# Experts' tokens gathered for two experts at a time, from high and low parts made by POOL, and the next expert's first gate product put between the two halves of the scatter

## What is computed

```python
def moe_swiglu(h, w_router, w_gate, w_up, w_down):
    logits = (h @ w_router).astype(jnp.float32)
    top_val, top_idx = lax.top_k(logits, TOP_K)              # 2 of 8
    top_w = jax.nn.softmax(top_val, axis=-1)
    gates = jnp.sum(jax.nn.one_hot(top_idx, N_EXPERTS) * top_w[..., None], axis=-2)
    out = jnp.zeros_like(h)
    for e in range(N_EXPERTS):
        y = (jax.nn.silu(h @ w_gate[e]) * (h @ w_up[e])) @ w_down[e]
        out = out + gates[..., e:e + 1] * y
    return out
```

## Time and profile before

| what | value |
|---|---|
| runs | 1834.43, 1839.47, 1834.2 us (median 1834.43) |
| profiled execution | 1839.33 us |
| its span | 1837.6 us, mean granted clock 0.989 |
| busy, of the span | PE 98%, DVE 76%, ACT 62%, POOL 6% |
| the experts' stage | from about 461 to 1448 us of the span |
| weights read | 476 MB by SP's queue |

### The profile page before, as it was taken

One profiled execution on the slowest core, in us unless ns is written; L12 is line 12 of the kernel. 1 busy time (PEld: TensorE's weight loads), 2 busy tenths in 40 slices (PEclk: granted clock), 3 DMA queues, 4 the chain that ended last, 5 costly groups with the idle time before them and its releaser, 6 DMA issues.

```text
span 1837.6 us, 25765 instructions
## 1 busy us (share of the span) xinstructions
PE 1794.9 (98%) x9992; PEld 1551.8 (84%) x9992; DVE 1405.8 (76%) x1164; ACT 1131.7 (62%) x942; POOL 116.7 (6%) x133
## 2 busy tenths in 40 slices
PE   8999999999999999999999999999999898899999
PEld 6789999898888888888888888888888797689998
DVE  6475445655988989898889888898898867677775
ACT  6444444463776777777777777767677544645553
POOL 7000000000000000000000000000000028210000
PEclk9999999999999999999999999999999999789999
DMA  7446565432998998998989989989999543225561
GB/s 234 161 139 196 172 206 183 161 138 81 356 386 310 388 367 323 385 369 324 375 329 375 368 321 385 368 327 381 343 355 370 199 141 135 69 86 189 184 200 54
DMA packets 244356, 479.27 MB, mean 261 GB/s; under 512 B 11759, under 2 KB 80137, under 8 KB 244249
## 3 DMA queue, kind: packets, MB, share of 16 engines
q1 hardware_dynamic: 243385, 476.43, 72.3%
q10 hardware_dynamic: 864, 1.31, 0.2%
HBM read 476.66 MB, written 1.05 MB: 260 GB/s over the span
## 4 chain that ended last, share of the span: by engine, by line
PE 89%; DVE 5%; POOL 2%; ACT 2%; issue 1%; DMA 0%; DVEq 0%; ACTq 0%; SPq 0%; POOLq 0%
PE bank L1978 28%; PE bank L1980 27%; PE bank L1979 27%; PE bank L2297 1%; PE bank L2329 1%; POOL arena L820 1%; DVE wl L438 1%; DVE xT L1295 1%; DVE xTl L1238 1%; POOL arena L821 1%; PE bank L2366 0%; PE bank L1947 0%; PE bank L2367 0%; DVE h L1308 0%; DVE xn L1251 0%
## 5 line engine op out<-in xcount | busy, mean ns | idle before, releaser
L1978 PE MATMUL bank<-wh,xTh 128*128 128x512 f32 x1568 | 622.2, 397 | 11.1 <-DVE arena L1334 5.4
L1980 PE MATMUL bank<-wh,xTl 128*128 128x512 f32 x1568 | 613.1, 391 | 0.0
L1979 PE MATMUL bank<-wl,xTh 128*128 128x512 f32 x1568 | 612.5, 391 | 0.0
L1542 DVE TENSOR_TENSOR wl<-raw,wh 128x2048 fp32r<-128x2048 f32 x224 | 512.1, 2290 | 92.6 <-ACT wh L1024 91.0
L1024 ACT ACTIVATE wh<-raw 128x2048 fp32r<-128x2048 f32 x224 | 429.2, 1918 | 120.7 <-PE bank L1980 120.7
L1978 PEld LDWEIGHTS bank<-wh,xTh 128*128 128x128 f32 x1568 | 295.8, 189 | 74.2 <-DVE arena L1334 5.6
L1980 PEld LDWEIGHTS bank<-wh,xTl 128*128 128x128 f32 x1568 | 295.6, 189 | 62.9
L1979 PEld LDWEIGHTS bank<-wl,xTh 128*128 128x128 f32 x1568 | 296.1, 189 | 58.6
L438 DVE TENSOR_TENSOR wl<-raw,wh 128x2048 fp32r<-128x2048 f32 x112 | 255.4, 2298 | 68.3 <-ACT wh L431 66.5
L1978 PE MATMUL bank<-xTh,wh 128*128 128x256 f32 x1024 | 292.1, 285 | 1.2 <-DVE xTl L1238 0.8
L1980 PE MATMUL bank<-xTh,wl 128*128 128x256 f32 x1024 | 290.9, 284 | 0.0
(11 more groups left out here) (379 smaller groups left out, 1397.3 us busy)
## 6 DMA issues: line engine op xcount, KB each, us to landing
raw<-in_moe_w_up SPq DMA_DIRECT2D x112, 1024.0 KB, 7.6
arena<-in_moe_w_gate SPq DMA_DIRECT2D x96, 1024.0 KB, 7.5
raw<-in_moe_w_down SPq DMA_DIRECT2D x96, 1024.0 KB, 7.1
raw<-in_w_up SPq DMA_DIRECT2D x22, 1024.0 KB, 5.8
raw<-in_moe_w_gate SPq DMA_DIRECT2D x16, 1024.0 KB, 7.4
arena<-in_moe_w_down SPq DMA_DIRECT2D x16, 1024.0 KB, 7.2
raw<-in_gla_w_in SPq DMA_DIRECT2D x12, 1024.0 KB, 8.0
raw<-in_w_in SPq DMA_DIRECT2D x12, 1024.0 KB, 6.2
```

Of the source, the lines that this page charges most:

```text
L1542: V.tensor_tensor(wl[:, s, :], moe_raw(c)[0], wh[:, s, :].bitcast(F32), ALU.subtract).then_inc(lo_moe, 1)
L1978: T.matmul(o, xh, yh, start=first, stop=False)
L1979: T.matmul(o, xh, yl, start=False, stop=False)
L1980: return T.matmul(o, xl, yh, start=False, stop=last)
```

## The change

- `oh` becomes `oh2`, which holds the one-hot matrices of two experts side by side (`slots(i)` picks one) in fp32r; the type is that of a second view `arena_r` of the same memory.
- POOL gets three new operations of 128 x 2048 right after the first gathers (`moe_xgfull` at 2): `xnh` is the tokens times the gain, as fp32r; `xn` is multiplied by the gain in place; `xnl` is `xn` minus `xnh`. The gain's row comes by a new DMA of 512 KB on ACT's queue, ahead of the one for `fgain`.
- `gather_pair` replaces the 14 later calls of `gather`. It runs once in a pair, after down of round 5 of the pair's first expert (i = 0), and makes the tokens of that pair's second expert and of the next pair's first: 4 banks x 2 channel blocks x 2 token tiles x (high, low), 32 fp32r matmuls of 128x256. It runs in the last pair too. The gain is in the operands already, so ACT and DVE split each bank straight from PSUM (four operations of 128x512 each, in a pair).
- The activations' high and low parts move from `xTh`/`xTl` to the arena.
- On PE the next expert's gate of round 0 moves from behind the scatter to between its halves. On DVE the last low part of an expert (`weights_lo(UC - 1)`) moves ahead of the last two additions to `h`.

```diff
@@ -74,7 +74,7 @@
         h = sb("h", [P, TT, D])
-        with nc.sbuf_tensor("ohT", [P, S], F32R) as ohT:
+        with nc.sbuf_tensor("xnh", [P, TT, D], F32R) as xnh:
@@ -84,7 +84,11 @@
         yh, yl = (a.rearrange("p a n -> p (a n)").rearrange("p (k s) -> p k s", s=S) for a in (acth, actl))
+        with nc.sbuf_tensor("xnl", [P, TT, D], F32R) as xnl:
+            pass
...
         xn = sb("xn", [P, TT, D])
+        with nc.sbuf_tensor("arena_r", [P, AR], F32R) as arena_r:
+            pass
@@ -122,6 +126,10 @@
+        def ar_r(n):
+            ar(n)
+            return arena_r[:, ar_at[0] - n:ar_at[0]]
@@ -453,6 +461,7 @@
         lo_moe = sg("lo_moe")
+        pair_banks = (0, 2, 3, 7)
@@ -528,15 +537,21 @@
         more_i = ar(1).bitcast(I32)
-        oh = ar(TT * P).rearrange("p (t s) -> p t s", t=TT)
+        oh2 = ar_r(TT * 2 * P).rearrange("p (t s) -> p t s", t=TT)
+        ohT = ar_r(S)
...
         ghot, gnow = ar(1), ar(TT)
-        xg = ar(KD * P).rearrange("p (k s) -> p k s", k=KD)
-        xgh, xgl = xTh[:, :, 0:P], xTl[:, :, 0:P]
-        eactTh, eactTl = xTh[:, :, P:S], xTl[:, :, P:S]
+        eactTh, eactTl = (ar_r(KD * P).rearrange("p (k s) -> p k s", k=KD) for _ in range(2))
+        gainrow = rs_home[:, 0:D]
...
         junk = arena[:, ar_at[0] - D:ar_at[0]]
-        assert 2 * EJ == D
+        assert 2 * EJ == D == KD * P
+        xg = junk.rearrange("p (k s) -> p k s", k=KD)
+        def slots(i):
+            return slice((1 - i % 2) * P, (2 - i % 2) * P)
@@ -799,6 +814,13 @@
             pool.wait_ge(sg("more_ready"), 1)
+            pool.wait_ge(sg("gr_in"), 16)
+            see(pool, "lg")
+            pool.wait_ge(sg("moe_xgfull"), 2)
+            gb = gainrow.unsqueeze(1).to_broadcast([P, TT, D])
+            G(V.tensor_tensor(xnh[:, :, :], xn[:, :, :], gb, ALU.mult))
+            G(V.tensor_tensor(xn[:, :, :], xn[:, :, :], gb, ALU.mult))
+            G(V.tensor_tensor(xnl[:, :, :], xn[:, :, :], xnh[:, :, :].bitcast(F32), ALU.subtract), "xn_split")
@@ -1036,17 +1058,15 @@
             A(V.activation(ex[:, :, :], ex[:, :, :], ACT.Exp), "rt_exp")
+            act.dma_start(gainrow, IN["ffn_norm"][1:2, :].to_broadcast([P, D])).then_inc(sg("gr_in"), 16)
...
-            def xg_hi(half, value):
-                act.wait_ge(sg("moe_xg"), value)
-                V.activation(xgh[:, 4 * half:4 * half + 4, :], xg[:, 4 * half:4 * half + 4, :], ACT.Copy).then_inc(sg("moe_xh"), 1)
...
             for half in range(2):
-                xg_hi(half, half + 1)
+                act.wait_ge(sg("moe_xg"), half + 1)
+                V.activation(xTh[:, 4 * half:4 * half + 4, slots(0)], xg[:, 4 * half:4 * half + 4, :],
+                             ACT.Copy).then_inc(sg("moe_xh"), 1)
@@ -1083,10 +1103,11 @@
                             V.activation(ohT[:, :], bank[7][:, 0:S], ACT.Copy).then_inc(sg("moe_ohT"), 1)
-                        if tail and (more_follow or i == 0):
-                            xg_hi(0, at(4, 2 * i + 3))
-                        if (kind, j, k) == ("d", NEJ - 1, 1) and (more_follow or i == 0):
-                            xg_hi(1, at(4, 2 * i + 4))
+                        if tail and i == 0:
+                            for n, b in enumerate(pair_banks):
+                                act.wait_ge(sg("moe_xgfull"), at(4, n + 3))
+                                V.activation(xTh[:, 2 * n:2 * n + 2, :], bank[b][:, :].rearrange("p (k s) -> p k s", k=2),
+                                             ACT.Copy).then_inc(sg("moe_xh"), 1)
@@ -1568,10 +1589,10 @@
-            def onehot(u, value):
+            def onehot(u, i, value):
...
+                V.tensor_tensor(oh2[:, :, slots(i)], iota2, pmu.unsqueeze(2).to_broadcast([P, TT, P]), ALU.is_equal).then_inc(sg("moe_oh"), 1)
@@ -1646,25 +1668,28 @@
                                 gates_now(at(2, i + 1))
-                                onehot(at(2, i + 1), at(2, i + 2))
-                        if (kind, j, k) == ("d", NEJ - 2, 1) and not last:
-                            gather_out(0, bank[7], at(4, 2 * i + 3))
-                            xg_lo(0, at(4, 2 * i + 3))
+                            if i == 0:
+                                for ii in (1, 2):
+                                    onehot(at(2, ii), ii, at(2, ii + 1))
+                        if (kind, j, k) == ("d", NEJ - 2, 1) and i == 0:
+                            for n, b in enumerate(pair_banks):
+                                ks = slice(2 * n, 2 * n + 2)
+                                dve.wait_ge(sg("moe_xh"), at(4, n + 3))
+                                V.tensor_tensor(xTl[:, ks, :], bank[b][:, :].rearrange("p (k s) -> p k s", k=2),
+                                                xTh[:, ks, :].bitcast(F32), ALU.subtract).then_inc(sg("moe_xl"), 1)
...
                     weights_lo(UC - 2)
-                    if not last:
-                        gather_out(1, bank[(NEJ * (i + 1) + 1) % 2], at(4, 2 * i + 4))
-                        xg_lo(1, at(4, 2 * i + 4))
...
                     for q in range(4):
+                        if q == 2:
+                            weights_lo(UC - 1)
...
                         V.tensor_tensor(hs, hs, bank[(7, 4, 5, 6)[q]][:, :], ALU.add).then_inc(sg("moe_h"), 1)
-                    weights_lo(UC - 1)
@@ -2294,9 +2319,20 @@
+            def gather_pair():
+                for n, b in enumerate(pair_banks):
+                    for k in range(2):
+                        ks = slice((2 * n + k) * P, (2 * n + k + 1) * P)
+                        for t in range(TT):
+                            for part in (xnh, xnl):
+                                ins = T.matmul(bank[b][:, k * S:(k + 1) * S], part[:, t, ks], oh2[:, t, :],
+                                               start=(t == 0 and part is xnh), stop=(t == TT - 1 and part is xnl))
+                    ins.then_inc(sg("moe_xgfull"), 1)
@@ -2305,22 +2341,34 @@
-            def experts(at, more_follow):
+            def experts(at, more_follow, first=False):
...
+                def gate_up(i, b, kind, j):
+                    for half in range(2):
+                        if kind == "g" and j == 0:
+                            pe.wait_ge(sg("moe_xl"), at(4, 4 + 2 * half) if i == 1 else at(4, 2 * i + 1 + half))
+                        h_, l_ = here(UC * i + upos[kind, j, half], 4)
+                        for k in range(4):
+                            kk = 4 * half + k
+                            ins = mm3(b[:, :], xTh[:, kk, slots(i)], xTl[:, kk, slots(i)], h_[:, k, :], l_[:, k, :],
+                                      kk == 0, kk == KD - 1)
+                        used(ins)
+                def gate(i, j):
+                    n = NEJ * i + j
+                    pe.wait_ge(sg("moe_act"), at(2 * NEJ, n + 1))
+                    gate_up(i, bank[n % 2], "g", j)
+                if first:
+                    gate(0, 0)
+                    return
...
-                    def gate_up(b, kind, j):
@@ -2369,13 +2417,13 @@
                         n = NEJ * i + j
-                        pe.wait_ge(sg("moe_act"), at(2 * NEJ, n + 1))
-                        gate_up(bank[n % 2], "g", j)
+                        if j:
+                            gate(i, j)
...
                             transposed(j - 1)
-                        gate_up(bank[2 + n % 2], "u", j)
+                        gate_up(i, bank[2 + n % 2], "u", j)
@@ -2383,31 +2431,30 @@
                     pe.wait_ge(sg("moe_ohT"), at(2, i + 1))
-                    if not last:
-                        pe.wait_ge(sg("moe_oh"), at(2, i + 2))
-                        gather(0, bank[7])
+                    if i == 0:
+                        pe.wait_ge(sg("moe_oh"), at(2, 3))
+                        pe.wait_ge(sg("xn_split"), 1)
+                        gather_pair()
...
                     last_down()
-                    if not last:
-                        pe.wait_ge(sg("moe_xg"), at(4, 2 * i + 3))
-                    else:
-                        pe.wait_ge(sg("moe_ghot"), at(2, i + 1))
+                    pe.wait_ge(sg("moe_ghot"), at(2, i + 1))
...
                     if not last:
-                        gather(1, bank[(NEJ * (i + 1) + 1) % 2])
+                        gate(i + 1, 0)
...
             pe.wait_ge(sg("more_ready"), 1)
+            experts(lambda a, b: b, True, True)
```

More of the change, by code:

```diff
@@ L1588, in xg_lo @@
                 dve.wait_ge(sg("moe_xh"), value)
-                V.tensor_tensor(xgl[:, hs, :], xg[:, hs, :], xgh[:, hs, :].bitcast(F32), ALU.subtract).then_inc(sg("moe_xl"), 1)
-            onehot(0, 1)
+                V.tensor_tensor(xTl[:, hs, slots(0)], xg[:, hs, :], xTh[:, hs, slots(0)].bitcast(F32),
+                                ALU.subtract).then_inc(sg("moe_xl"), 1)
+            onehot(0, 0, 1)
             C(V.tensor_reduce(cmax[0:1, 0:1], see(dve, "cnt")[0:1, 0:NE], AX.X, ALU.max), frees="cnt")
@@ L2296, in gather @@
                     for t in range(TT):
```

(21 more changed lines are left out.)

1 line of the change is left out of this document (removed).

## The result

The changed kernel takes 1848.75 us (median of 4 runs, 1847.58 to 1849.30). The kernel before takes 1834.95 us on the same chip (4 runs, 1834.20 to 1839.47). The ratio is 1.0069, with a 95% interval of 1.0052 to 1.0087, so the change is slower by 0.7%. The forecast was 1837.7 us with a range of 1825 to 1843: **the prediction was wrong**, on the slow side. Its profiled execution took 1848.46 us, span 1846.4 us.

A forecast was written before the change was run, and what follows sets the result against it. The prediction took PE, busy for all of an expert's 123.87 us, as the bound. Gathers -11.1, POOL's hold on DVE +11.6 and clock +2.8 made +3.3 us on 1834.43: 1837.7 us, range 1825 to 1843.

The forecast's parts named there:

- about 122 us on average: Sign of a right forecast: experts from the second on take about 122 us on average, before 123.9.
- PE's gathers: Changes of expert: 14 gathers (25.1 us) and small waits (1.4) go, four gather_pair runs (15.4) come: -11.1 us.
- The gate between the halves: Change of expert: the moved gate (5.5 us) covers ACT's eyh and DVE's eyl of the scatter's second half; no gain counted.
- POOL holding DVE up: Start of the experts' stage: POOL's three operations delay DVE, so PE stalls 2.3 and 9.3 us: +11.6 us.
- The first rival: Start of the experts' stage: POOL holds DVE up not at all or only partly; 1823.3 us, partial cases to 1829; chance 0.22.
- the low end of its range: 1831.5 us: a PE stall of 8.5 us without a clock fall, slack taking some 3.7 of 12.3 us.
- The clock: First expert, behind the 9.3 us stall: PE runs at 1.2 GHz for a while, 13 matmuls slow, with the ramp +2.8 us.
- The second rival: First expert, pieces 2 to 6: clock stays low 13.5 us after the stall, losing 6.3 us; 1841.2 us; chance 0.15.
- The DMA bound: Experts' stage: weight DMA holds no more than 356 GB/s, so the 11.1 us gain does not come; 1848.8 us; chance 0.03.

The follow-up runs named there:

- the kernel with the swap: The changed kernel with POOL's work cut into twelve operations, activations' parts in xT's memory and xnh in the arena: 1827.01 us against 1837.42 for the kernel before.

## Why the prediction was wrong

**The failed step** is an edit with no term in the sum: the activations' high and low parts go from `xTh` and `xTl` to the arena. The text ahead of the prediction names the move, and the prediction costs the new operands of the gathers ("changes nothing in the form") but says nothing of this one; it was taken as a change of names. The offset in the arena was not worked out. It cost 10 to 11 us, and it is the whole miss: 11.3 us at most by the spacing, 10.9 by the pairs, alone on the kernel before 9.8 us in the stage and 10.7 on the medians (1847.95 - 1837.22). With the block aligned the change comes out at +1.4 us in the stage and -0.9 us on the medians, where +3.3 had been forecast. The prediction asked for experts of "about 122 us on average"; 246.65 / 2 = 123.3 was the first sign in the profile, and the spacing of the matmuls the second. Aligned, an expert takes 122.0.

**PE's gathers: right.** `gather_pair` takes 3.74 us (forecast 32 x 0.12 = 3.84). A pair gains 3.84 to 3.88 us where PE's spacing is as before (forecast 3.7).

**The gate between the halves: right.** It hides the wait for `eyl`, as the prediction said; put behind the scatter it costs 9.3 us.

**POOL holding DVE up: right, a little large.** Two waits were forecast, 2.3 us for `xTl` and 9.3 us for `wl`, and two or three DVE operations of 4 to 5 us. There are 1.8 and 7.25 us, and operations of 3.69 and 4.53 us and two merged in one row of 4.34 us. The term was 11.6 us; PE is 10.9 us late. By the Trainium skill (SBUF — State Buffer, "SBUF: two separate sides") the pair of ports that the two engines share is held for the whole instruction, and the other engine blocks. These rows agree: the operation on 16 columns took 4.53 us beside POOL's of 4.89. The first rival (POOL does not hold DVE up) is refuted by the rows. The 12.3 us with which the prediction worked out the low end of its range is derived nowhere in it; the forecast does not use it.

**The clock: right in kind, somewhat large.** The term was 2.8 us behind the stall and came out at 1.6, 8 matmuls and not 13; in the aligned kernel it was 2.2 and 11. In the changed kernel the fall came earlier than thought: from 466.82 us on, matmuls of piece 1 started 0.43 us apart, behind the wait of 1.82 us and ahead of the long one. Those 1.8 us are part of the 10.9 above. The second rival, the clock low for 13.5 us behind the stall, did not come about: it is 1.00 from 480.3 on.

**The DMA bound: refuted,** although its figure, 1848.8 us, is almost the measured one. No row has ACT waiting for a piece, and the kernel with the swap moves 363 GB/s through a whole pair, more than the 356 at which the rival put the ceiling. A time that agrees is no evidence for its mechanism.

## What to carry to other kernels

Where a change moves an operand that TensorE loads as weights, work out its byte offset in the partition and keep it at a multiple of 256 for blocks of 128 four-byte columns (no other size of block was tried); look at the start-to-start spacing of the matmuls, not at their mean duration, since 5.7 to 6.6 ns on each down matmul cost 7 to 11 us here, 0.4 to 0.6% of the program. Large two-input POOL operations beside a busy DVE are cut up and spread over rounds that have slack (13.3 us won here), and not put where DVE is the next thing that PE waits for. List every edit of a diff with its own term, also one that only gives a tensor another home.

## What was not expected of the hardware

- The start of the stationary block: 226.7 ns from matmul to matmul at a multiple of 256 or 512 bytes, 232.4 at a multiple of 128 only, 233.3 at 8 bytes past a multiple of 64. The weight loads' own listed durations hardly differ: 189 to 190 ns on average in the changed kernel, 188 in the aligned ones. How the weights are fetched, so that this comes out, no run here shows. Other alignments were not tried. The offsets are worked out from the order and sizes of the allocations.
- With the start 8 bytes off, the gate's and up's matmuls, whose operands had not moved, also started further apart: the gate's 227.7 against 226.7, up's 228.1 against 227.9 on average. Why is open.
- A wait of 1.82 us for PE was followed by matmuls at the lower clock, 0.43 us apart, from 1.6 us after its restart on. The same came in two other kernels with POOL's whole operations at the start, but not in the one with the block aligned to 512 bytes, whose wait was as long. What decides is open.
- POOL's two-input operations on 2048 columns took 4.5 to 4.9 us while DVE's waiting operations were small, and 5.9 to 6.5 us while DVE did its large subtractions.
